# A third group of seven products per half of the down projections, with two of its sums made by adding transfers, and an earlier preparation of the first unit

## The reference

```
x = x + 0.5 * post1(SwiGLU_1(pre1(x)))          # FFN width 5632
u = pre_mix(x); [MLA inputs | MoBA q,k,v] = u @ W_in
y = W_out(concat[RMSNorm(MLA heads), RMSNorm(MoBA heads)])
x = x + post_mix(y)
x = x + 0.5 * post2(SwiGLU_2(pre2(x)))
def swiglu(x, w_gate, w_up, w_down):
    return (silu(x @ w_gate) * (x @ w_up)) @ w_down
```

## Time and profile before

| | |
|---|---|
| time, median of 3 runs | 1765.66 us |
| the profiled execution | 1764.84 us, of which the span of the instructions is 1763.2 us |
| PE busy | 1738.4 us (99%), granted clock 0.998 of full |
| DVE busy | 1411.3 us (80%) |
| ACT busy | 1000.9 us (57%) |
| POOL busy | 64.3 us (4%) |
| DMA | 389.75 MB, mean 221 GB/s |

### The profile page before, as it was taken

One profiled execution on the slowest core, in us unless ns is written; L12 is line 12 of the kernel. 1 busy time (PEld: TensorE's weight loads), 2 busy tenths in 40 slices (PEclk: granted clock), 3 DMA queues, 4 the chain that ended last, 5 costly groups with the idle time before them and its releaser, 6 DMA issues. The chain is left out here.

```text
span 1763.2 us, 21394 instructions
## 1 busy us (share of the span) xinstructions
PE 1738.4 (99%) x7968; PEld 1442.9 (82%) x7968; DVE 1411.3 (80%) x1284; ACT 1000.9 (57%) x979; POOL 64.3 (4%) x99
## 2 busy tenths in 40 slices
PE   9999999999999999999999999999999999999998
PEld 8788888888888888888888877788888888888886
DVE  6888888888888888665578558888888888888887
ACT  6656665555655654543347446555566666555563
POOL 0000000000000000010000000000000000000000
PEclk9999999999999999999999999999999999999999
DMA  9677787777765554355441446777777787666453
GB/s 387 224 264 250 253 261 244 238 238 241 243 236 220 188 214 176 137 225 189 175 162 52 188 174 255 262 239 238 245 251 241 251 251 244 233 235 239 170 195 112
DMA packets 58978, 389.75 MB, mean 221 GB/s; under 512 B 6432, under 2 KB 6688, under 8 KB 16160
## 3 DMA queue, kind: packets, MB, share of 16 engines
q1 hardware_dynamic: 52720, 344.77, 50.9%
q0 software_dynamic: 6048, 44.04, 13.0%
q10 hardware_dynamic: 144, 0.04, 0.0%
HBM read 384.63 MB, written 4.19 MB: 221 GB/s over the span
## 5 line engine op out<-in xcount | busy, mean ns | idle before, releaser
L2084 PE MATMUL banks<-w_hi,act_hi 128*128 128x512 f32 (+1 forms) x1088 | 425.2, 391 | 1.6 <-DVE w_lo L1343 1.2
L2086 PE MATMUL banks<-w_hi,act_lo 128*128 128x512 f32 (+1 forms) x1088 | 421.5, 387 | 0.0
L2085 PE MATMUL banks<-w_lo,act_hi 128*128 128x512 f32 (+1 forms) x1088 | 421.2, 387 | 0.0
L1384 DVE TENSOR_TENSOR op_lo<-quads,op_hi 128x2048 fp32r<-128x2048 f32 x140 | 318.7, 2289 | 43.1 <-ACT op_hi L918 42.2
L918 ACT ACTIVATE op_hi<-quads 128x2048 fp32r<-128x2048 f32 x140 | 266.6, 1918 | 53.8 <-PE banks L2086 33.7
L2278 PE MATMUL banks<-w_hi,hid_split 128*128 128x512 f32 x992 | 275.1, 389 | 0.5 <-DVE hid_split L1607 0.5
L1373 DVE TENSOR_TENSOR w_lo<-raw,w_hi 128x2048 fp32r<-128x2048 f32 x80 | 181.4, 2288 | 80.9 <-ACT w_hi L892 80.7
L1343 DVE TENSOR_TENSOR w_lo<-raw,w_hi 128x2048 fp32r<-128x2048 f32 (+3 forms) x67 | 143.9, 2147 | 124.7 <-ACT w_hi L843 124.7
L2084 PEld LDWEIGHTS banks<-w_hi,act_hi 128*128 128x128 f32 x1088 | 204.6, 188 | 43.4 <-DVE w_lo L1343 2.2
L2086 PEld LDWEIGHTS banks<-w_hi,act_lo 128*128 128x128 f32 x1088 | 204.3, 188 | 41.8
L2085 PEld LDWEIGHTS banks<-w_lo,act_hi 128*128 128x128 f32 x1088 | 204.7, 188 | 40.0
(11 more groups left out here) (209 smaller groups left out, 2331.3 us busy)
## 6 DMA issues: line engine op xcount, KB each, us to landing
raw<-in_weights SPq DMA_DIRECT2D x203, 1024.0 KB, 4.9
quads<-in_paired SPq DMA_DIRECT2D x80, 1024.0 KB, 7.8
quads<-in_paired POOLq DMA_DIRECT2D x40, 1024.0 KB, 8.4
raw<-in_paired SPq DMA_DIRECT2D x32, 768.0 KB, 6.0
rows<-in_x SPq DMA_DIRECT2D x4, 1024.0 KB, 11.7
raw<-in_weights SPq DMA_DIRECT2D x6, 512.0 KB, 3.6
gain_row<-in_post_gains SPq DMA_DIRECT2D x3, 1024.0 KB, 6.5
raw<-in_weights SPq DMA_DIRECT2D x4, 768.0 KB, 4.1
```

The source lines that it names most:

```text
L1384: nc.vector.tensor_tensor(op_lo[:, slot, :], op_raw(op), op_hi[slot][:, :], ALU.subtract)\
L2084: nc.tensor.matmul(out_ap, hi, rhs_hi, start=start, stop=False, skip_group_check=chain)
L2085: nc.tensor.matmul(out_ap, hi, rhs_lo, start=False, stop=False, skip_group_check=chain)
L2086: return nc.tensor.matmul(out_ap, lo, rhs_hi, start=False, stop=stop, skip_group_check=chain)
```

## The change

The number of groups of seven products per half goes from 2 to 3 (`D_GROUPS` 4 to 6) and the plain pieces of a stage from 32 to 26 (`DP`). How many products stand behind each piece is a table, up to two. `op_split` gets two slots, the second laid over `rows`, whose reload therefore moves to the end of the stage. `sum1` and `sum2` of a down group leave DVE: POOL issues two adding transfers, the second from SBUF to SBUF. The signs of the left side change to fit, which gives `sum_sides` one more instruction. In the gate/up stages `join_split` moves ahead, the four multiplications (`norm_pairs`) come before the seventh piece's low part and the sums (`sum_pairs`) behind it, ACT's first copy waits for the multiplications alone, and L4 is loaded before quadrant R22.

```diff
-DP = 32
+DP = 26
-D_GROUPS = 4
+D_GROUPS = 6
+GAPS = {(0, 0): (1,) + (2,) * 9 + (1, 1, 0), (0, 1): (2,) * 9 + (1, 1, 1, 0),
+        (1, 0): (1,) + (2,) * 9 + (1, 1, 0), (1, 1): (2,) * 10 + (1, 0, 0)}
+def products_behind(down, half, p):
+    first = D_HALF * half + sum(GAPS[down, half][:p])
+    return range(first, first + GAPS[down, half][p])
+def product_slot(down, n):
+    half, k = n // D_HALF, n % D_HALF
+    return 0 if half and not down and k == D_HALF - 2 else k % 2
...
# SP: load_unit, load_units
-                sp.wait_ge(op_lo_ready, per_unit(stage, v.u, 3, OP_COUNT[O_P7]))
-                load_quad(stage, ahead, R22)
                 sp.wait_ge(lo_ready, made(stage, v.u, L2))
                 load_plain(stage, v, L4)
+                sp.wait_ge(op_lo_ready, per_unit(stage, v.u, 3, OP_COUNT[O_P7]))
+                load_quad(stage, ahead, R22)
...
# SP: load_behind
+                if op == O_P7:
+                    sp.wait_ge(down_lo_ready, down_step(stage, n))
+                    sp.wait_ge(down_sum2_landed, down_step_sum(stage, group))
+                    load_down_quad(stage, group + 1, R22)
...
# POOL
+            def add_down_quads(stage, half):
+                for group in range(D_GROUPS // 2 * half, D_GROUPS // 2 * (half + 1)):
+                    row = 8 * (UNITS - 1) + 4 * (D_GROUPS * down(stage) + group) + R11
+                    pool.wait_ge(down_sum_ready, down_sum(stage, group, 1))
+                    nc.gpsimd.dma_start(down_quad(R12), paired[row, :, 0:D_OPERAND]
+                                        .rearrange("p (a n) -> p a n", a=D_PAIRS), accum_op=ALU.add)\
+                      .then_inc(down_sum1_landed, 16)
+                    nc.gpsimd.dma_start(down_quad(R11), down_quad(R22), accum_op=ALU.add).then_inc(down_sum2_landed, 16)
...
# ACT: gate_up, down_operand_high, down_proj
-                act.wait_ge(norm_step, 5 * ffn(stage) + 5)
+                act.wait_ge(norm_step, 5 * ffn(stage) + 2)
...
+                if slot_used_by(down(stage), n) is not None:
+                    act.wait_ge(down_used, down_step(stage, slot_used_by(down(stage), n)))
...
+                        act.wait_ge(down_sum1_landed if op == O_P5 else down_sum2_landed, down_step_sum(stage, group))
...
+                    if half == 0:
+                        down_operand_high(gu_stage, stage, D_HALF)
                         take_pair_down(stage, HALF)
                         square_down(stage, 0)
                         take_pair_down(stage, HALF + 1)
...
# DVE: gate_up
+                if stage == GU2:
+                    join_split(stage)
                 take_low(piece(stage + 4))
+                if stage == GU1:
+                    join_split(stage)
...
-                join_split(stage)
+                norm_pairs(stage)
                 take_low(piece(stage + 6))
-                norm_pairs(stage)
+                sum_pairs(stage)
                 take_low(piece(stage + 7))
                 split_pairs(stage)
...
# DVE: down_sum4, end_first, down_proj
+                dve.wait_ge(down_sum2_landed, down_step_sum(stage, group))
+                nc.vector.tensor_tensor(down_quad(R21), down_quad(R21), down_quad(R11), ALU.add)\
...
+                dve.wait_ge(tile0_done, tiles_before(stage) + HALF * half + HALF - 2)
...
+                        if plain:
+                            take_low_down(pc)
+                        for i, n in enumerate(products_behind(down(stage), half, p)):
+                            if n % D_HALF:
+                                down_operand_low(stage, n)
+                            if n % D_HALF == D_HALF - 1:
+                                end_second(stage, half)
+                            if plain and i == 0:
+                                hid_low_down(stage, pc, ahead)
+                            if n % D_HALF == D_HALF - 1:
+                                if final:
+                                    take_low_last(down_piece_of(DOWN2, DP - 1))
+                                end_third(stage, half)
+                            behind_operand(stage, n)
...
# PE: down_proj
+                    for p in range(HALF):
+                        if not (stage == DOWN2 and half and p >= HALF - 2):
+                            down_piece(stage, HALF * half + p, mixed if not half and not p else None)
+                        if half == 0 and p == 1:
                             turn_hidden(gu_stage, N_FB - 1)
+                        for n in products_behind(down(stage), half, p):
+                            down_product(gu_stage, stage, n)
```

More of the change, by code:

```diff
@@ L494, in down_sum, with down_step_sum @@
         def down_sum(stage, group, k):
-            return 4 * (D_GROUPS * down(stage) + group) + k
+            return 2 * (D_GROUPS * down(stage) + group) + k
+        def down_step_sum(stage, group):
+            return 16 * (D_GROUPS * down(stage) + group + 1)
         def side(stage, group, k):
@@ L778, in step, with inverse_rms @@
                 pool.wait_ge(var_ready, steps[0])
-            def inverse_rms(job, parts, width, factor, col=0):
+            def inverse_rms(job, parts, width, factor, col=0, run=None):
                 c = factor ** -2
-                for n in range(parts):
+                for n in range(parts) if run is None else run:
                     for t in range(TILES):
@@ L817, in _ @@
             add_all_quads(GU1)
-            inverse_rms(R_POST1, 2, D, 0.5)
+            for half in range(2):
+                add_down_quads(DOWN1, half)
+                inverse_rms(R_POST1, 2, D, 0.5, run=(half,))
             inverse_rms(R_PRE_MIX, 1, D, 1.0)
@@ new lines, in down_proj @@
+                for half in range(2):
+                    for p in range(HALF):
+                        ahead = HALF * half + p + 1
+                        plain = 1 <= p < HALF - 1 and not (stage == DOWN2 and ahead == DP - 1)
+                        if plain:
+                            take_high_down(down_piece_of(stage, ahead))
+                        for i, n in enumerate(products_behind(down(stage), half, p)):
+                            if n % D_HALF:
+                                down_operand_high(gu_stage, stage, n)
+                            if plain and i == 0:
+                                hid_high_down(down_piece_of(stage, ahead), ahead)
+                            if n == 2:
+                                keep_hidden(gu_stage, N_FB - 2, N_FB - 1)
+                            behind_operand(stage, n)
+                        if plain and not products_behind(down(stage), half, p):
+                            hid_high_down(down_piece_of(stage, ahead), ahead)
+                    if half == 0:
+                        down_operand_high(gu_stage, stage, D_HALF)
@@ L1692, in end_second @@
                 base = 4 * (2 * down(stage) + half)
[L1693 removed]
+                dve.wait_ge(down_used, down_step(stage, D_HALF * half + D_HALF - 2))
                 end_sum(stage, half, 2, O_P6, 1, 0)
@@ L1779, in down_proj, with behind_operand @@
                         take_both_down(stage, HALF + 1)
+            def behind_operand(stage, n):
+                group, op = down_group(n), D_ORDER[n % len(D_ORDER)]
+                at_end = (group + 1) % (D_GROUPS // 2) == 0
+                if op == O_P1 and n:
+                    side_low(stage, group, SIDE_SUMS)
+                elif op == O_P3:
+                    down_sum3(stage, group)
+                    side_low(stage, group, SIDE_REST)
+                elif op == O_P5:
+                    down_sum4(stage, group)
+                elif op == O_P6:
+                    if at_end:
+                        end_first(stage, n // D_HALF)
+                    if group < D_GROUPS - 1:
+                        sum_sides(stage, group + 1)
+                elif op == O_P4 and not at_end:
+                    side_low(stage, group + 1, SIDE_A11)
             def rotate(to, of, table, n_heads, half):
@@ L2286, in down_product @@
                 group, op, half = down_group(n), D_ORDER[n % len(D_ORDER)], n // D_HALF
+                slot = product_slot(down(stage), n)
                 pe.wait_ge(down_lo_ready, down_step(stage, n))
```

264 lines of the change are left out of this document (112 added, 152 removed).

## The result

| | time, us (median; lowest to highest) | ratio to before, 95% interval |
|---|---|---|
| before | 1765.2 (1764.6 to 1766.0) | |
| changed | 1801.2 (1798.9 to 1803.5) | 1.0200 (1.0185 to 1.0215) |

The change costs 36 us where 4 were forecast as a gain, and the time lies outside the range of 1750 to 1776. Slower had been given 0.28, and the mechanism is the one of rival 2, at a higher price than it had there.

The account below looks back on a forecast made before the run. PE, busy 1738.4 of 1763.2 us, was taken as the bound. Terms -8.2 - 9.5 + 4.6 + 3.3 + 0.7 + 2.8 + 2.0 = -4.3 us gave a forecast median of 1761.3 us, range 1750 to 1776.

Parts of the forecast that it names:

- rival 2: Down stages: the second adding transfer is late, making the kernel slower, 1779 us at 15 us and 1789 at 16; chance 0.27.
- the adding transfers' term: Down stages: waits for the two adds, second sum taken as ready 12 us after down_sum3; +2 us, bounds 0 and +14.
- the sign that I had named: Down stages: an SBUF add landing beyond 13 us after issue, DVE idle before down_sum4 in every group, would show rival 2.
- the tight groups: Down groups with pairs (P3, P2), (P7, P5), (P6, P4), first and fifth of a stage: 11.2 and 11.9 us before PE waits.
- the loose ones: Down groups in the other alignment, three or four a stage: 14 us before PE waits; 2 us lost each at 16.
- break points: Down groups: sum lateness from which PE waits for P4, 11.2 and 11.9 us in one alignment, 14 in the other.
- Fewer matmuls: Down halves: 3 pieces (72 matmuls) become 7 products (63), 36 matmuls fewer over four halves; -8.2 us.
- starts: Start of each down stage: +0.4 at piece 0 and +1.9 at product 2; +4.6 us for both, bounds +3 and +6.
- seams: Between a down stage's halves: +1.3 and +1.0 against 0.6 lost now, +1.6 a stage; +3.3 us in all.
- ends: End of DOWN1 +0.7 us; end of DOWN2 +2.2 at the last product and +0.6 for the join, +2.8 us.
- Units' beginnings: First units of GU1 and GU2: stalls at 49.00, 55.73, 88.65 and 95.04 and their repeats go; -9.5 us, -9.8 at most.
- DVE at 91%: Steady down groups: DVE has 30.4 us of work per 33.3 us of PE and fits; 0, at most 2 us a stage.

Follow-up runs that it names:

- e1_ring: The changed kernel with more room for POOL's transfer descriptors (SCRATCH 1536 instead of 1024, the pad smaller by as much): 1792.8 us.
- e5_third: The changed kernel with the second adding transfer taking one of its three pairs of rows, the rest of that sum left out: 1764.0 us.
- e2_begin: The kernel before with the units' part alone (gate/up preparation order and L4 loaded before R22), down stages as before: 1759.1 us.
- e8_noadd: The changed kernel without adding transfers in the down stages, both sums made by DVE: 1773.7 us.

## Why the prediction was wrong

- **The step that failed is the adding transfers' term**, "The sum is ready 10 to 15 us after `down_sum3`; I take 12". It was ready after 13.9 to 16.7, 14.7 by the median, and cost not 2 us but 37 (1801.2 against 1764.0 with the sum in time). The time: I took the second transfer to need some 5 us behind the first. The two are served one after the other, at 6.9 and 6.5 us, which was my upper bound; the issue that POOL could make only when the first had landed adds 0.6 us to that (e1_ring; 8.4 us of the time) and is not the main reason. So the sign that I had named, an SBUF add landing beyond 13 us after its issue, did not show in the changed kernel (6.2 to 9.2), and did in e1_ring. My estimate of 6.5 us for an add of 768 KB was near (6.9), but the 2.6 us before the first byte in it are shown by no row; in the trace of the kernel before an add's first packet starts 1.5 to 1.8 us after its issue. The price: the term's bound of +14 at 15 us counted the tight groups alone, while rival 2, at the same 15 us, counted the loose ones too, 20 us.
- **Its break points.** The forecast had 11.2 and 11.9 us for the tight groups and 14 for the others. In the four tight groups the sum was there after 15.5, 15.2, 15.2 and 15.6 us, and PE lost 1.27 + 2.49, 1.02 + 2.50, 1.01 + 2.51 and 1.37 + 2.53 us, 14.7 in all, where those points give 15.2: sized right. Two of the loose ones, at 15.6 and 16.7 us, lost 1.32 and 2.51, also as by the rule. With each group's own landing the rule gives 20 us instead of 2, some 1779, and the chip took 22 more. What it lacked I read from the trace against that of e5_third, in PE's stalls in the down stages (38.3 us against 12.8) and its clock: 5.2 us before the next groups' first operands, 2.9 of them the two stalls before P1 that are shown above; 1.7 us more at the seams; 5.9 us of clock; and a longer first matmul behind each of 19 more stalls (0.5 instead of 0.39, some 0.1 each), 2 us. That leaves about 4 of the 37 us unplaced. On top, against the forecast, the units' part gave 6.6 instead of 9.5.
- **The clock was in no term.** The changed kernel's windows around one of its stalls (PE resumes at 673.13 after 2.50 us):
```profile
660.00:672.00 12.00, 9.61 (x41) 7.26 (x40) 9.35 (x10) 5.70 (x5) 0.00 (x0) 1.00 0.80 257
672.00:678.00 6.00, 4.87 (x14) 3.91 (x15) 5.03 (x4) 2.81 (x3) 0.00 (x0) 0.72 0.81 291
678.00:690.00 12.00, 12.00 (x54) 9.91 (x53) 12.00 (x10) 8.55 (x8) 0.89 (x1) 1.00 0.51 126
```
PE stands still for 2.5 us, and the granted clock goes from its upper level (2.4 GHz) to the lower (1.2 GHz) for part of the next window: 0.72 over 6 us loses 1.7 us. It happens four times where the kernel before has none: at the stalls at 673.13, 1575.45, 1736.26 and 1776.05; 7 us. Not every such stall brings it (515.44 with 2.49 us and 1645.57 with 2.51 did not).
- **Fewer matmuls, starts, seams, ends: right, to 1.7 us.** The third of the second add, which leaves just these terms, measures them against the units' part alone: 1764.0 - 1759.1 = +4.9 us; the forecast had -8.2 + 4.6 + 3.3 + 0.7 + 2.8 = +3.2. The stalls stand where forecast: 1.50 us at product 2 (forecast 1.9), 1.21 and 0.61 at the seam (1.3 and 1.0), 2.00 and 0.31 at the end (2.2 and 0.6). The remaining 1.7 us are the size of one dip of the clock, and e5_third has one, at 1048 to 1052 us, that the kernel before has not; that this is the cause wasn't tested. So the third group was a loss by the forecast's own terms even with the transfers free, and I had covered that with the units' gain.
- **Units' beginnings: right in kind, too high.** -6.6 against -9.5. The stalls at 49.00 and 55.73 went. L4 came sooner, ACT began on it at 80.02 instead of 83.06, but some 9.8 us after its issue (e2_begin), where 9.3 was the latest that costs nothing: a stall of 0.55 stayed at 85.61 (0.38 and 0.54 in e2_begin). And the stalls of 0.7 at 95.04 and in GU2, which I had hung on the same chain, stayed: that step was wrong. In e2_begin the four that stayed, 0.38, 0.54, 0.69 and 0.69 us, with 0.15 for each first matmul, are the 2.9 us that were missing.
- **DVE at 91%: right.** In e5_third, where DVE has the work of the forecast and the transfer is in time, it is busy for 210.97 of 234.20 us of DOWN1, 90%, and PE has only the forecast's stalls. With one sum more it is 94% and still holds; at 96% (e8_noadd) it doesn't.

## What to carry to other kernels

An adding transfer whose sum the next step needs is priced by the moment at which it is there: measure that, and the latest moment that costs nothing, before anything else; here 10 us cost nothing and 12.4 cost 13. Two such transfers behind each other add up, in the queue's room or in the transfer itself. And with an engine that is 94% busy behind the one that sets the pace, a stall taken away by another order mostly came back at a later product: here only the one at the very end, with no product behind it, went for good.

## What the hardware showed beside that

- POOL issued a second adding transfer 0.6 us behind the first where its queue had room (e1_ring), and waited 6.2 us for the first's landing where it hadn't. With a third of the bytes, in one run of 2 KB per partition instead of three, the unchanged room was enough (e5_third).
- Two adds of 768 KB take as long side by side (13.1 us from the second's issue) as one behind the other (6.9 and 6.5). A third of the second's bytes takes 9.0, two thirds 11.5: about 2 us for each 256 KB on top of what the first has left. POOL's own share of that is small: it is busy with the two issues for 0.86 and 1.64 us in e1_ring.
- The Trainium skill ("DMA: Bandwidth & Descriptors", section "Anatomy of one DMA — SWDGE (gpsimd) path") has 2.0 us plus bytes over 436 GB/s, which for 768 KB gives 3.8 us as an estimate by that page. The adds took 6.9 and 6.5 us by the median, beside SP's own loads, so the trace does not agree for adding transfers.
